# HGRN's levels issued in pairs over two PSUM banks, the keys' turn joined to the two largest levels, and the last keys and queries written in place

## The reference

```
k = (1 - lb) * sigmoid(-z);  f = lb + (1 - lb) * sigmoid(z);  q = silu(hq) * 128 ** -0.5
S_t = diag(f_t) S_{t-1} + k_t^T v_t;    o_t = S_t^T q_t          (T = 16 meta tokens + 512)
o = rmsnorm(o) * silu(hg)
```

## Time and profile before

| | |
|---|---|
| runs, us | 2636.61, 2634.43, 2634.19; median 2634.43 |
| profiled execution | 2636.31 us, span of its records 2634.4 us |
| granted TensorE clock, mean | 0.998 |
| TensorE matmul, share of the span | 99% |
| TensorE weight loads | 88% |
| VectorE | 52% |
| ScalarE | 39% |
| GpSimd | 2% |

### The profile page before, as it was taken

How to read it: one execution, slowest core, us unless ns; L and a number is a source line. 1 busy time by engine, 2 the same in 40 slices (tenths; PEclk the granted TensorE clock), 3 DMA queues, 4 the chain that set the end, 5 groups by cost and what they waited for, 6 DMA issues and landing times.

```text
span 2634.4 us, 42702 instructions
## 1 busy us (share of the span) xinstructions
PE 2596.0 (99%) x18898; PEld 2321.8 (88%) x18898; DVE 1359.3 (52%) x2196; ACT 1038.9 (39%) x1700; POOL 40.2 (2%) x90
## 2 busy tenths in 40 slices
PE   9999999999999999999999999999999999999998
PEld 7777888888887788888899899999999989999998
DVE  6766533324656543333567446555336754655533
ACT  4554422213545442221455344344224534543421
POOL 0000000000100000000000000000000000000000
PEclk9999999999999999999999999999999999999999
DMA  5221222222312122222231222222223113222222
GB/s 189 88 67 62 82 95 96 92 99 81 110 64 79 65 96 96 96 90 88 95 103 51 74 91 95 83 95 93 89 90 124 66 58 105 90 88 97 93 89 76
DMA packets 39865, 235.75 MB, mean 89 GB/s; under 512 B 5520, under 2 KB 7824, under 8 KB 17536
## 3 DMA queue, kind: packets, MB, share of 16 engines
q1 hardware_dynamic: 34912, 214.45, 23.9%
q0 software_dynamic: 4048, 17.00, 2.0%
q10 hardware_dynamic: 720, 1.57, 0.2%
HBM read 222.38 MB, written 6.42 MB: 87 GB/s over the span
## 4 chain that ended last, share of the span: by engine, by line
PE 94%; DVE 3%; ACT 2%; DMA 0%; issue 0%; SPq 0%; DVEq 0%; ACTq 0%
PE P L535 78%; PE P L627 3%; PE P L649 3%; PE P L542 2%; PE P L661 1%; PE P L885 1%; DVE WL L1809 1%; PE P L675 1%; PE P L998 1%; PE P L906 1%; PE P L707 1%; ACT WH L1245 0%; PE P L1048 0%; DVE X L1941 0%; DMA X<-in_xT 0%; PE P L1050 0%
## 5 line engine op out<-in xcount | busy, mean ns | idle before, releaser
L535 PE MATMUL P<-XH,WL 128*128 128x264 f32 (+3 forms) x3080 | 844.2, 323 | 17.1 <-DVE XL L1958 6.0
L535 PE MATMUL P<-XL,WH 128*128 128x264 f32 (+3 forms) x3080 | 823.0, 316 | 0.0
L535 PE MATMUL P<-XH,WH 128*128 128x264 f32 (+3 forms) x3080 | 820.5, 315 | 0.0
L1809 DVE TENSOR_TENSOR WL<-raw,WH 128x1024 fp32r<-128x1024 f32 (+1 forms) x403 | 482.6, 1201 | 529.4 <-ACT WH L1245 528.8
L1245 ACT ACTIVATE WH<-raw 128x1024 fp32r<-128x1024 f32 (+1 forms) x403 | 417.3, 1039 | 597.8 <-PE P L535 595.6
L535 PEld LDWEIGHTS P<-XH,WL 128*128 128x128 f32 x3080 | 520.4, 188 | 66.6 <-DVE XL L1958 8.0
L535 PEld LDWEIGHTS P<-XH,WH 128*128 128x128 f32 x3080 | 519.0, 189 | 37.9
L535 PEld LDWEIGHTS P<-XL,WH 128*128 128x128 f32 x3080 | 518.8, 188 | 36.8
L2479 DVE SCALAR_TENSOR_TENSOR tmp<-P,PP,tmp 128x527 f32<-128x527 f32 (+1 forms) x88 | 66.8, 759 | 195.3 <-ACT tmp L1754 195.3
L535 PE MATMUL P<-GHH,WL 128*128 128x264 f32 (+1 forms) x704 | 149.1, 283 | 0.0
L535 PE MATMUL P<-GHL,WH 128*128 128x264 f32 (+1 forms) x704 | 148.9, 282 | 0.0
(11 more groups left out here) (344 smaller groups left out, 3414.2 us busy)
## 6 DMA issues: line engine op xcount, KB each, us to landing
raw<-in_wts SPq DMA_DIRECT2D x169, 1024.0 KB, 4.9
raw<-in_wts SPq DMA_DIRECT2D x32, 896.0 KB, 4.6
spill<-X POOLq DMA_DIRECT2D x2, 2112.0 KB, 9.3
X<-spill POOLq DMA_DIRECT2D x16, 264.0 KB, 3.0
qswap<-qraw SPq DMA_DIRECT2D x44, 64.0 KB, 2.0
tab<-in_tR POOLq DMA_DIRECT2D x2, 1056.0 KB, 5.3
tmp<-in_biasT POOLq DMA_DIRECT2D x16, 128.0 KB, 3.2
tmp<-in_biasT POOLq DMA_DIRECT2D x16, 112.0 KB, 2.7
```

The source lines that it names most:

```text
L535: ins = nc.tensor.matmul(P[:, a:a + x1 - x0], wb[:, s, 128 * k:128 * k + 128], xb[:, kx, x0 - c0:x1 - c0], start=start and i == 0, stop=st ...
L1809: nc.vector.tensor_tensor(WL[:, u % NS, 0:length(u)], raw[:, u // 2 % RAW, a:a + length(u)], WH[:, u % NS, 0:length(u)].bitcast(F), ALU.su ...
```

## The change

On TensorE a head's six levels become three stops: levels -1 and 0 in step 2, 1 and 2 in step 4, 3 and 4 in step 6, with steps 3, 5 and 7 empty. The second pair is written to bank 5, the others to bank 4; the two levels of a pair lie beside each other in the bank (`level_area`). Each level still has its own waits for its preparation and its own signal; the bank is taken once and given back when the second is merged. The turn moves from step 9 into step 8, behind the two block levels. On VectorE step 2 makes the preparations of levels 1 and 2, step 3 merges -1 and 0; step 4 prepares 3 and 4, step 5 merges 1 and 2; step 6 prepares 5 and 6, step 7 merges 3 and 4 and makes the last keys and queries. Those go into K and Q themselves and no longer into `KBs[1]` and `QAs[1]`, and no longer wait for the block levels' matmuls. On ScalarE the two copies of the turned keys move from step 9 into step 8, ahead of the three copies of the block levels. The silu of a head's queries waits for the output matmul of the head two before, since Q is now read until then. The number of instructions and their shapes stay as they are.

```diff
--- before.py
+++ after.py
@@ -210,6 +210,11 @@
 
     return Threads((lru(), 10, 30, 94), (hgrn(0), 16, 1, 57), (hgrn(1), 16, 54, 102), (hgrn(2), 16, 98, 146), (hgrn(3), 16, 145, 193),
                    (ret_scores(), 6, 112, 142), (ret_values(), 8, 157, 185), (ret_gate(), 3, 182, 197), (lru_gate(), 3, 188, 206))
+
+
+def level_area(lev):
+
+    return (2560 if lev in (1, 2) else 2048) + 144 * ((lev + 1) % 2)
 
 
 def one(b):
@@ -986,22 +991,25 @@
             def hgrn(l, h):
                 Q = Qs[h % 2]
                 yield
-                for lev in range(-1, 5):
-                    b = lev % 2
-                    qa, kb = (Q, hK) if lev < 0 else (QAs[b], hK if lev == 0 else KBs[b])
-                    pe.wait_ge(*at("hp", l, h, lev))
-                    pe.wait_ge(*at("hq", l, h))
-                    take(4)
-                    for j in range(4):
-                        for r in range(0, 128, 32):
-                            c, o = META + 128 * j + r, 2048 + 32 * j
-                            ins = nc.tensor.matmul(P[r:r + 32, o:o + 32], kb[:, c:c + 32], qa[:, c:c + 32],
-                                                   start=(j == 0), stop=(j == 3), skip_group_check=True)
-                    if lev < 4:
-                        ins = nc.tensor.matmul(P[0:16, 2176:2192], kb[:, 0:16], qa[:, 0:16], start=False, stop=True,
-                                               skip_group_check=True)
-                    ins.then_inc(*pe.up("hs", l, h, lev))
-                    give((4,), ("hc", l, h, lev))
+                for low in (-1, 1, 3):
+                    b = 5 if low == 1 else 4
+                    take(b)
+                    for lev in (low, low + 1):
+                        qa, kb = (Q, hK) if lev < 0 else (QAs[lev % 2], hK if lev == 0 else KBs[lev % 2])
+                        area = level_area(lev)
+                        pe.wait_ge(*at("hp", l, h, lev))
+                        pe.wait_ge(*at("hq", l, h))
+                        for j in range(4):
+                            for r in range(0, 128, 32):
+                                c, o = META + 128 * j + r, area + 32 * j
+                                ins = nc.tensor.matmul(P[r:r + 32, o:o + 32], kb[:, c:c + 32], qa[:, c:c + 32],
+                                                       start=(j == 0 and lev == low), stop=(j == 3), skip_group_check=True)
+                        if lev < 4:
+                            ins = nc.tensor.matmul(P[0:16, area + 128:area + 144], kb[:, 0:16], qa[:, 0:16], start=False, stop=True,
+                                                   skip_group_check=True)
+                        ins.then_inc(*pe.up("hs", l, h, lev))
+                    give((b,), ("hc", l, h, low + 1))
+                    yield
                     yield
                 pe.wait_ge(*at("hp", l, h, 6))
                 take(4)
@@ -1016,14 +1024,14 @@
                                                start=(j == 0 and b == 64), stop=(j == 3), skip_group_check=True)
                 ins.then_inc(*pe.up("hs", l, h, 6))
                 give((4,), ("hsc", l, h))
-                yield
                 pe.wait_ge(*at("hp", l, h, 7))
                 take(5)
-                nc.tensor.transpose(P[0:16, 2944:3072], KBs[1][:, 0:16], ident)
+                nc.tensor.transpose(P[0:16, 2944:3072], hK[:, 0:16], ident)
                 for j in range(3):
-                    ins = nc.tensor.transpose(P[:, 2560 + 128 * j:2688 + 128 * j], KBs[1][:, META + 128 * j:META + 128 * j + 128], ident)
+                    ins = nc.tensor.transpose(P[:, 2560 + 128 * j:2688 + 128 * j], hK[:, META + 128 * j:META + 128 * j + 128], ident)
                 ins.then_inc(*pe.up("ht", l, h))
                 give((5,), ("hkt", l, h))
+                yield
                 yield
                 pe.wait_ge(*at("hkt", l, h))
                 pe.wait_ge(*at(f"v{h // 2}", l, 2))
@@ -1047,7 +1055,7 @@
                     for a, b in segments(c0, c0 + 128):
                         nc.tensor.matmul(P[:, o + a:o + b], VI[:, 1 + j, v], SC[:, a - META:b - META],
                                          start=(a == 264), stop=False, skip_group_check=True)
-                        ins = nc.tensor.matmul(P[:, o + a:o + b], S[:, j, :], QAs[1][:, a:b], start=False, stop=True,
+                        ins = nc.tensor.matmul(P[:, o + a:o + b], S[:, j, :], Q[:, a:b], start=False, stop=True,
                                                skip_group_check=True)
                 ins.then_inc(*pe.up("hpv", l, h))
                 give((6, 7), ("ho", l, h))
@@ -1564,17 +1572,17 @@
                 for r in range(0, 128, 32):
                     nc.scalar.activation(scd[r:r + 32, :, r:r + 32], SD[r:r + 32, 0:128].rearrange("p (j c) -> p j c", c=32), ACT.Copy
                                          ).then_inc(*act.up("hsd", l, h, r))
+                act.wait_ge(*at("ht", l, h))
+                if h:
+                    act.wait_ge(*at("hkv", l, h - 1))
+                nc.scalar.activation(KT[:, 0:384], P[:, 2560:2944], ACT.Copy).then_inc(*act.up("hkt0", l, h))
+                nc.scalar.activation(KT[0:16, 384:512], P[0:16, 2944:3072], ACT.Copy).then_inc(*act.up("hkt", l, h))
                 act.wait_ge(*at("hs", l, h, 6))
                 pb = bank(4).rearrange("p (j c) -> p j c", c=128)
                 for i, (r0, r1, c) in enumerate(((0, 32, 32), (64, 96, 96), (0, 64, 64))):
                     nc.scalar.activation(scd[r0:r1, :, c:c + r1 - r0], pb[r0:r1, :, c:c + r1 - r0], ACT.Copy
                                          ).then_inc(*act.up(*(("hsc", l, h) if i == 2 else ("hs6", l, h, i))))
                 yield
-                act.wait_ge(*at("ht", l, h))
-                if h:
-                    act.wait_ge(*at("hkv", l, h - 1))
-                nc.scalar.activation(KT[:, 0:384], P[:, 2560:2944], ACT.Copy).then_inc(*act.up("hkt0", l, h))
-                nc.scalar.activation(KT[0:16, 384:512], P[0:16, 2944:3072], ACT.Copy).then_inc(*act.up("hkt", l, h))
                 yield
                 yield
                 act.wait_ge(*at("hpv", l, h))
@@ -1674,7 +1682,7 @@
                 def hq(u, p, h):
                     act.wait_ge(*at("unit", u))
                     if h >= 2:
-                        act.wait_ge(*at("hp", l, h - 2, 7))
+                        act.wait_ge(*at("hpv", l, h - 2))
                     nc.scalar.activation(Qs[h % 2][:, :], pair_bank(p), ACT.Silu).then_inc(*act.up("hq", l, h))
 
                 def hg(u, p, h):
@@ -2248,7 +2256,8 @@
 
                 def merge(lev):
                     n = 144 if lev < 4 else 128
-                    nc.vector.copy_predicated(SD[:, 0:n], masks[:, lev + 1, 0:n], P[:, 2048:2048 + n]).then_inc(*dve.up("hc", l, h, lev))
+                    a = level_area(lev)
+                    nc.vector.copy_predicated(SD[:, 0:n], masks[:, lev + 1, 0:n], P[:, a:a + n]).then_inc(*dve.up("hc", l, h, lev))
 
                 dve.wait_ge(*at("hf", l, h))
                 dve.wait_ge(*at("lb", l))
@@ -2261,10 +2270,15 @@
                 dve.wait_ge(*at("hz", l, h))
                 prep(0)
                 yield
-                for lev in range(-1, 5):
-                    dve.wait_ge(*at("hs", l, h, lev))
-                    if lev == -1:
-                        if h:
+                for low in (-1, 1, 3):
+                    prep(low + 2)
+                    prep(low + 3)
+                    yield
+                    for lev in (low, low + 1):
+                        dve.wait_ge(*at("hs", l, h, lev))
+                        if lev >= 0:
+                            dve.wait_ge(*at("hc", l, h, lev - 1))
+                        elif h:
                             dve.wait_ge(*at("hpv", l, h - 1))
                             dve.wait_ge(*at("hsd", l, h - 1, 96))
                         else:
@@ -2272,16 +2286,14 @@
                             nc.vector.memset(SC[:, :], 0.0).then_inc(*dve.up("hz1", l))
                             nc.vector.memset(SD[:, :], 0.0).then_inc(*dve.up("hz2", l))
                             dve.wait_ge(*at("hz2", l))
-                    else:
-                        dve.wait_ge(*at("hc", l, h, lev - 1))
-                    merge(lev)
-                    prep(lev + 2)
-                    yield
-                dve.wait_ge(*at("hs", l, h, 6))
+                        merge(lev)
+                    if low < 3:
+                        yield
                 dve.wait_ge(*at("hA", l, h, 6))
-                nc.vector.tensor_tensor(KBs[1][:, 0:META + 384], K[:, 0:META + 384], B[:, 0:META + 384], ALU.mult
+                nc.vector.tensor_tensor(K[:, 0:META + 384], K[:, 0:META + 384], B[:, 0:META + 384], ALU.mult
                                         ).then_inc(*dve.up("hp", l, h, 7))
-                nc.vector.tensor_tensor(QAs[1][:, META:T], Q[:, META:T], A[:, META:T], ALU.mult).then_inc(*dve.up("hd1", l, h, 7))
```

(2 more changed lines are left out.)

## The result

The changed kernel takes 2643.81 us (median of 8 runs, 2640.12 to 2645.67) beside 2636.51 us for the kernel before (8 runs, 2634.19 to 2639.2). The ratio is 1.0026, interval 1.0017 to 1.0035: 7.3 us slower. The forecast was 2.5 us slower, and the measured time lies 1.1 us above the top of the range. The kernel before now stands 2.1 us above the median of three runs from which the forecast started, and 7.3 us on that old base would be 2641.7, inside the range. So it is the base that puts the time outside; what was wrong in the forecast itself is the difference, 7.3 against 2.5.

What follows compares the result with a forecast made beforehand. The prediction took TensorE, busy 2596.0 of 2634.4 us, as the bound. Pairs -5.8, the turn -0.4 and new waits +8.7 summed to +2.5 us, a forecast of 2636.9 us, range 2630.9 to 2642.7.

Steps and rivals of the forecast that it cites:

- The bound and the path: Whole kernel: TensorE is the bound, busy 2596.0 of 2634.4 us, and each new wait on it is time of the whole.
- Part 1, pairs: TensorE, block levels: six stops per head become three, 24 pairs saving 0.24 us each, 5.8 us less (4.6 to 7.2).
- Rival 2: Second level of each pair: TensorE empties there as at a stop, pairs save nothing, 2642.7 us; chance 0.06.
- Rival 4: Whole kernel: no net change, the drains worth 8.0 us, 2634.7 us; chance 0.62 shared with the forecast.
- Part 2, the turn: Turn of the keys joined to the two largest block levels: only an exit saved, 0.4 us less (0 to 1.0).
- Part 3, the waits: VectorE prepares twice, then merges twice: new TensorE waits of 4.35 us per layer, 8.7 in all (6.8 to 11.6).
- Head 0: Step 2: level 0 is wanted before its queries are written, wait 0.4 us (0.3 to 0.5).
- Head 1: Step 8, bank 4: free before TensorE wants it, no wait, with 0.15 us in hand (0 to 0.4).
- rival 1: Merge of the largest level: bank 4 held in head 1 too and longer in head 2, 2641.2 us; chance 0.2.
- Head 2: Step 8, bank 4: VectorE is the slower and frees it late, wait 0.95 us (0.5 to 1.5).
- Head 3, bank 5: Retention's first state product waits for VectorE to free the bank, 3.0 us (2.6 to 3.4), the largest wait.
- rival 3: Head 3: VectorE clears bank 5 before retention asks, -3.5 us, 2630.9 us; chance 0.12.

Runs made afterwards that it cites:

- experiment 5: Changed kernel with head 3's second pair in bank 4 and, in head 2 alone, levels 3 and 4 merged ahead of the preparations: 2631.19 us, ratio 0.9982.
- experiment 6: experiment 5 with levels -1 and 0 in two stops again, 8 pairs of 24 undone: 2632.74 us.
- the repeat: The changed kernel run again unaltered, beside two versions of the kernel before with shorter added waits: 2643.28 us, ratio 1.0023.
- experiment 1: Also called bank4_head3: changed kernel with head 3's second pair back in bank 4, so retention does not wait for bank 5: 2633.57 us, ratio 0.9989.
- experiment 4: Kernel before, VectorE's merge of level 2 in head 3 delayed by four multiplications and retention's first product made to wait for it: 2644.95 us, ratio 1.0032.
- merge_first: Also called experiment 2: changed kernel, VectorE merges ahead of preparations in every head, last keys and queries moved into step 6: 2640.18 us, ratio 1.0012.
- before_wait_2us: Kernel before, merge of level 2 in head 3 delayed by two multiplications and retention's first product made to wait for it: 2641.56 us, ratio 1.0021.
- first_pair_apart: Also called experiment 3: merge_first with levels -1 and 0 of each head in two stops again: 2640.67 us.
- experiment 7: experiment 5 with the turn of the keys back in step 9, on TensorE and ScalarE: 2633.05 us.
- experiment 8: merge_first with the last keys and queries in step 7, behind retention's second sums: 2632.86 us.

## Why the prediction was wrong

- **The bound and the path**: right. TensorE sets the time throughout, and each new wait is time of the whole, with nothing to hide it.
- **Part 1, pairs**: right. 24 pairs at 0.24 us was 5.8; the runs give 0.245 and 0.26 per pair, some 6.3 with the turn. A single undisturbed pair shows 0.29. Why the average is a little lower was not broken down; head 0's largest level, in the shorter stream, cost only 0.48 as a stop of its own and had less to give. By the fixed latency of the Trainium skill, "TensorE: Matmul & The Clock Gate", Single matmul latency, a pair would have saved 0.33; that estimate was too high. Rival 2 (pairs save nothing) falls with experiments 5 and 6. Its number, +8.3 or 2642.7 us, lies near the measured one for another reason and is no point in its favour. Rival 4 (no net change, the drains worth 8.0 us) falls too: the pairs save 6 and the time rose by 7.3.
- **Part 2, the turn**: right, 0.4 forecast, 0.3 to 0.8 measured.
- **Part 3, the waits**: right in each place. Head 0: 0.4 forecast, 0.25 measured. Head 1: none and none, so rival 1 falls. Head 2: 0.95 and 1.3. Head 3, bank 5: 3.0 and 3.1, so rival 3 falls. The sum was 8.7 and is 9.4.
- **The step that failed**: "Behind those waits on TensorE stands only the stream, so each is time of the whole." That prices a wait at its own length. In the profile of the changed kernel the stream and retention's product run at 1.2 GHz for some 6 us behind the 3.1 us wait, which costs 2.6 and 2.9 us more in the two layers, about 5 in all (in the repeat 1.5 and 2.4, about 4); the prediction has no term for it. Without it the terms give 9.4 - 6.3 = +3.1 us, near the forecast. With it they give +8.2, and the profiled mixers show 3.99 + 4.28 = 8.27 (the medians 7.3: most of the runs had a mean clock of 0.996 or 0.997, the profiled one 0.995). That the clock follows the wait is shown twice: with the wait gone from the changed kernel the time falls by 10.2 us (experiment 1), and with a wait of 2.8 us alone in the kernel before it rises by 8.9 (experiment 4).

The sign was in the trace of before, in a stretch that the prediction did not look at. The timeline of TensorE there, with the longest wait ahead of a mixer:

```profile
1315.13 0.39 PE L535 MATMUL P<-XH,WL 128*128 128x264 f32 x1 [2.71 <-DVE XL L2021]
```

and the windows over it and behind it:

```profile
1312.00:1316.00 4.00, 1.29 (x9) 0.88 (x9) 2.57 (x7) 2.56 (x6) 0.04 (x1) 1.00 0.96 406
1316.00:1320.00 4.00, 4.00 (x23) 4.00 (x22) 3.50 (x10) 1.70 (x4) 0.43 (x1) 0.57 0.32 135
```

A wait of 2.7 us, and 0.57 of the clock in the 4 us behind it. It is not a rule: the trace of before has two more waits of over 2 us, one of 2.06 at 198.5 with 0.57 behind it (200 to 204) and one of 2.13 at 228.2 with 1.00 behind it (230 to 234). But a new wait of 3.0 us should have been given such a tail as a likely term: 0.43 of 4 us, 1.7 us each, 3.4 in all, which would have put the forecast at about 2640 and raised the chance of slower.

## What to carry to other kernels

Price a new wait on a dense TensorE stream at its length plus what the clock does behind it, and take that tail from the windows behind the longest waits that the trace already has. It is a term with a chance, not a sure one. A change that pairs work on the bound engine also pairs it on the engine that feeds it: look at what now stands between the signal and the release of the buffer, as here two preparations and two low halves ahead of a merge. Moving the release to the front is a change of order like the first, and whatever it pushes back (here retention's second sums) has to be looked at in the same way.

## What was not expected of the hardware

- **The clock behind a wait is no matter of the wait's length alone.** Behind the new waits of 0.9 and 1.3 us it did not fall in any profile taken. Behind 1.8 and 1.9 us it fell in four cases of six: in one layer of two in merge_first and before_wait_2us, in both in first_pair_apart. Behind the new 2.8 and 3.1 us waits it fell in all six cases profiled. But behind the old 2.7 us wait ahead of the first mixer it fell in six of the 13 profiles, among them the kernel before and the changed one (0.57 and 0.58), and not in the other seven, though the code there is the same in all. The windows of bank4_head3, one of the seven:

```profile
1314.00:1318.00 4.00, 1.29 (x9) 0.88 (x8) 2.48 (x7) 2.54 (x6) 0.10 (x1) 1.00 0.95 401
1318.00:1322.00 4.00, 4.00 (x34) 4.00 (x33) 3.59 (x10) 1.72 (x5) 0.34 (x1) 1.00 0.33 139
```

  A short wait is not safe either: in the changed kernel's profile the clock is 0.59 from 268 to 272, behind two old waits of 0.95 and 0.63 us that stand 2 us apart. What decides between these is open; no run here was made for it.
- **It makes the time scatter.** Where a kernel has a wait at which the clock sometimes falls, its runs spread over 6 to 9 us (experiments 2, 3 and before_wait_2us), against 3 to 4 us in experiments 1 and 5 to 8. The kernel before, with its old waits, lies between: 5.3 us over 33 runs. A median of few runs then says little of an edit worth 1 us.
- **Small matmuls of 16 columns cost next to nothing between others of their form.** Those of the first level overlap with the next level's, 0.04 us from start to start.
